# The first two score steps of a dilated attention, issued before the last half of the value projection

## The chip, the cores and the metric

The kernel runs on one core of a Trainium2 chip. Its time is the device time of one execution in microseconds (us). Five engines work side by side: PE multiplies matrices, ACT (ScalarE) applies functions and copies, DVE (VectorE) and POOL (GpSimd) work element by element, and SP starts the transfers from memory. Each engine runs its own instructions in the order in which they were written, and waits on counters (semaphores) that other engines raise.

## The reference

Two model blocks run one after the other over 512 tokens of width 1024. The second block holds, as its second layer, a dilated attention with three groups (window and dilation differ) of eight heads each; the change lies in it alone.

```python
def dilated_attention_mixer(h, positions, w_qkv, w_o):
    qkv = (h @ w_qkv).reshape(b_, s_, 3, g_ * hh, dh)
    q = partial_rotary(qkv[:, :, 0], positions).reshape(b_, s_, g_, hh, dh)
    k = partial_rotary(qkv[:, :, 1], positions).reshape(b_, s_, g_, hh, dh)
    v = qkv[:, :, 2].reshape(b_, s_, g_, hh, dh)
    for g, (window, dilation) in enumerate(DILATED_PATTERNS):
        o_g, lse_g = dilated_window_attention(q[:, :, g], k[:, :, g], v[:, :, g], window, dilation)
    weights = jax.nn.softmax(jnp.stack(lses, axis=0), axis=0)
    o = jnp.sum(weights[..., None] * jnp.stack(outs, axis=0), axis=0)
    return o.reshape(b_, s_, hh * dh).astype(h.dtype) @ w_o
```

Each group's outputs are weighted by the share of its sum of exponentials in the sum over the three groups, so that the kernel takes one softmax over the 768 scores that a block of 128 queries has in the three groups together.

## The kernel before

**The weights.** All weights come as 216 slabs of 1 MB (`w_stage`). POOL splits each slab into a high part (`w_high`, line 410) and a low part (`w_low`, line 415), four instructions each; there are two buffers, and a slab is split into the buffer of the slab before the last as soon as PE has done with that one (`slab_done`). PE makes each product out of three matmuls (lines 473 to 475, function `triple`).

**The attention.** The heads are done in two batches of four. For each batch PE takes twelve slabs of queries and keys, which DVE scales, rotates and stores in `qk2` (named qk in rows of the profile; `head_ready` counts them), and then six slabs of values, two halves for each group `g`. The four banks 4 to 7 of `psum` hold a group's values for the four token blocks `c`; they are complete when the second half is, and ACT then copies each of them to `v_tok` (lines 1252 and 1253), which raises `drained[4 + c]`.

**The steps.** Then come 16 steps of a batch (`t`, four heads by four blocks of queries). For each step
- PE computes the scores into two of the banks 0 to 3 (lines 920 to 922; even steps take 0 and 1, odd steps 2 and 3),
- DVE adds the mask and takes the row maxima (lines 1790 to 1798) into `sc2` (named scores in rows),
- ACT takes the exponential (line 1260),
- DVE divides by the sum (lines 1778 and 1779),
- PE transposes the six blocks of probabilities into banks 4 and 5 (line 945),
- ACT copies them out (`pt2`, line 1268),
- PE multiplies them with the values (line 936).

PE's order in one round `t` is scores of `t`, values of `t - 2`, transposes of `t - 1`. DVE's order is division of `t - 1`, maxima of `t`. ACT's order is exponential of `t`, copy of `t - 1`. Ahead of the first round PE waits for the batch's heads and for `drained` of banks 7, 1, 3 and 5: for bank 7, that is the copy of the last block of values.

Of the kernel before, what the change touches and what calls it, by code (L numbers as in the profile page):

```python
# [28 lines left out]
ACT = mybir.ActivationFunctionType  # L29
# [3 lines left out]
P = 128  # L33
# [8 lines left out]
GROUPS, GHEADS = 3, 8  # L42
BATCH_HEADS = 4
# [113 lines left out]
def build(nc, a):  # L157

    ctx = ExitStack()
    with ctx:  # L160
# [309 lines left out]
        def _(pe):  # L470
# [394 lines left out]
            def attn(p):  # L865
                s0 = p.slab
                for batch in range(2):

                    j0 = 18 * batch
                    if batch == 0:  # L870
                        first_slab(p, (0, 1))
                        plain_slab(p, 1, (2, 3), attn_high, attn_low)
                        turn_rstd(p, 6)
                        done = 2
                    else:
                        done = 0
                    base = [p.drain[b] + used[b] for b in range(4)]
                    if batch:
                        pe.wait_ge(drained[0], base[0])
                        pe.wait_ge(drained[2], base[2])  # L880
                    rounds = (12 - done) // 2
                    with pe.Fori(0, rounds) as i:
                        for r in range(2):
                            s = s0 + j0 + done + r
                            pe.wait_ge(slab_split, i * 2 + (s + 1))
                            slab_two_tiles(s % 2, (2 * r, 2 * r + 1), lambda b: pe.wait_ge(drained[b], i + base[b]), attn_high, attn_low)
                    for b in range(4):
                        used[b] += rounds

                    for g in range(GROUPS):  # L890
                        for half in range(2):
                            s = s0 + j0 + 12 + 2 * g + half
                            pe.wait_ge(slab_split, s + 1)
                            for c in range(TOK):
                                if half == 0:
                                    take(p, 4 + c)
                                for k in range(4):
                                    kk = 4 * half + k
                                    last = triple(ps[:, 4 + c, :], ah[:, kk, c * P:(c + 1) * P], al[:, kk, c * P:(c + 1) * P],
                                                  wh[:, s % 2, k * 512:(k + 1) * 512], wl[:, s % 2, k * 512:(k + 1) * 512],  # L900
                                                  kk == 0, kk == 7)
                                if half == 1 and c < 3:
                                    last.then_inc(tile_done, 1)
                            last.then_inc(slab_done, 1)

                    steps = BATCH_HEADS * DIL
                    n0 = MIX_STEPS + steps * batch
                    pe.wait_ge(head_ready, MIX_HEADS + 24 * (batch + 1))
                    pe.wait_ge(drained[7], p.drain[7] + used[7])
                    pe.wait_ge(drained[1], p.drain[1] + used[1])  # L910
                    pe.wait_ge(drained[3], p.drain[3] + used[3])
                    pe.wait_ge(drained[5], p.drain[5] + used[5])
                    for t in range(steps + 2):
                        if t < steps:
                            h, r = divmod(t, DIL)
                            b = 2 * (t % 2)
                            take(p, b)
                            q = [qk2[:, 4 * g + h, r * P:(r + 1) * P] for g in range(GROUPS)]
                            k = [qk2[:, 12 + 4 * g + h, :] for g in range(GROUPS)]
                            pe.matmul(ps[:, b, :], q[0], k[0], start=True, stop=True)  # L920
                            pe.matmul(ps[:, b + 1, 0:P], q[1], k[1][:, r * P:(r + 1) * P], start=True, stop=True)
                            pe.matmul(ps[:, b + 1, P:2 * P], q[2], k[2][:, r * P:(r + 1) * P], start=True, stop=True) \
                                .then_inc(scores_done, 1)
                        if t >= 2:
                            n = t - 2
                            h, r = divmod(n, DIL)
                            pe.wait_ge(drained[4], p.drain[4] + 19 * batch + 3 + n + 1)
                            b = 6 + h % 2
                            if r == 0:
                                take(p, b)  # L930
                            for kb in range(6):
                                if kb < 4:
                                    v = v2(0, kb)[:, h * P:(h + 1) * P]
                                else:
                                    v = v2(kb - 3, r)[:, h * P:(h + 1) * P]
# [12 lines left out]
                out_projection(p, tiles(o2h), tiles(o2l), lambda k: pe.wait_ge(split_low, split_base_attn() + k + 1))  # L948
# [15 lines left out]
        def _(act):  # L964
# [275 lines left out]
            def attn(p):  # L1240
# [4 lines left out]
                for batch in range(2):  # L1245
                    t0 = p.tile + 21 * batch + 12
                    s0 = p.slab + 18 * batch + 12
                    for g in range(GROUPS):
                        for c in range(TOK):
                            act.wait_ge(*((tile_done, t0 + 3 * g + c + 1) if c < 3 else (slab_done, s0 + 2 * g + 2)))  # L1250
                            if batch == 0:
                                act.wait_ge(drained[6], p.drain[6] + 1)
                            act.activation(v2(g, c), ps[:, 4 + c, :], ACT.Copy, scale=stat[:, 12 + c:13 + c]) \
                                .then_inc(drained[4 + c], 1)
                    steps = BATCH_HEADS * DIL
                    n0 = MIX_STEPS + steps * batch
                    for t in range(steps + 1):
                        if t < steps:
                            act.wait_ge(max_ready, n0 + t + 1)
                            act.activation(sc2[:, t % 2, :], sc2[:, t % 2, :], ACT.Exp, scale=P ** -0.5,  # L1260
                                           bias=stat[:, t % 2:t % 2 + 1], accum_out=stat[:, 2 + t % 2:3 + t % 2]) \
                                .then_inc(exp_ready, 1)
                        if t >= 1:
                            n = t - 1
                            act.wait_ge(probs_turned, n0 + n + 1)
                            if n >= 2:
                                act.wait_ge(values_done, MIX_VALUES + steps * batch + n - 1)
                            act.activation(pt2[:, (n % 2) * 768:(n % 2 + 1) * 768],
                                           ps[:, 4:6, :].rearrange("p b c -> p (b c)")[:, 0:768], ACT.Copy) \
                                .then_inc(drained[4], 1)  # L1270
                            if n % DIL == 2 and n > DIL:
                                o2_copy(p, batch, n // DIL - 1)
                    if batch == 1:

# [702 lines left out]
```

## Time and profile before

| | |
|---|---|
| median of 3 runs (lowest to highest) | 2667.6 us (2667.1 to 2673.45) |
| the profiled execution | 2669.08 us |
| its span in the trace | 2667.3 us |
| PE busy | 2597.1 us, 97% of the span |
| POOL, DVE, ACT busy | 66%, 41%, 19% |
| granted TensorE clock, mean | 0.988 of full speed |

The span runs from the first to the last instruction that the trace shows; the execution has 1.78 us around it. A busy share of 97% says that PE is nearly always at work, not that all of that work has to stand where it stands, and time in which PE runs at the lower clock counts as busy. So two things are read beside it: PE's idle stretches with what ended them, and the granted clock behind them. The clock has two levels here, 2.4 GHz (1.00 in the rows) and 1.2 GHz (0.50).

### The profile page before, as it was taken

How to read it: one execution, taken by the hardware profiler on the slowest of the kernel's cores; microseconds unless marked ns; L12 is line 12 of the kernel's file. 1: busy time of each engine (PE TensorE's matmuls, PEld its weight loads, DVE VectorE, ACT ScalarE, POOL GpSimd, SP SyncE). 2: the span in 40 equal slices, each digit the busy share in tenths (PEclk: the TensorE clock that was granted, in tenths of full speed). 3: DMA queues.
4: the chain of work that ended last, by engine and by line, in shares of the span. 5: the costliest groups of instructions: out<-in, count | busy, mean ns of one | idle time of the engine just before them, and what ended most of it. 6: DMA issues, size and time to landing. Idle time of an engine off the chain costs nothing.

```text
span 2667.3 us, 32279 instructions
## 1 busy us (share of the span) xinstructions
PE 2597.1 (97%) x11906; PEld 2138.4 (80%) x11906; DVE 1082.2 (41%) x1730; ACT 500.6 (19%) x843; POOL 1747.7 (66%) x1761
## 2 busy tenths in 40 slices
PE   7989999999899999999999999999999999999997
PEld 6768888887688888888888888888788878888885
DVE  4753322037533320443521504872567055503325
ACT  3432111034321110201100104100400143100022
POOL 5637777666377776777776876777257615867763
PEclk9999999999999999999999999999999999999998
DMA  4112222231122222222222223223012202222221
GB/s 154 48 48 95 94 96 103 100 117 48 48 95 94 94 95 99 91 99 105 103 95 95 94 95 105 93 97 108 33 63 94 96 31 87 94 95 95 95 95 63
DMA packets 36893, 236.71 MB, mean 89 GB/s; under 512 B 4049, under 2 KB 5585, under 8 KB 9169
## 3 DMA queue, kind: packets, MB, share of 16 engines
q1 hardware_dynamic: 33456, 230.78, 24.7%
q10 hardware_dynamic: 3360, 4.85, 0.6%
q8 instruction: 56, 0.92, 0.1%
q14 instruction: 21, 0.16, 0.0%
HBM read 233.51 MB, written 2.10 MB: 88 GB/s over the span
## 4 chain that ended last, share of the span: by engine, by line
PE 95%; DVE 2%; ACT 1%; issue 1%; POOL 0%; DMA 0%; DVEq 0%; SPq 0%; POOLq 0%; ACTq 0%
PE psum L473 29%; PE psum L474 29%; PE psum L475 29%; PE psum L936 2%; PE psum L920 1%; PE psum L684 1%; PE psum L945 1%; PE psum L798 1%; PE psum L814 0%; PE psum L503 0%; DMA x_res<-in_x 0%; PE psum L830 0%; PE psum L520 0%; PE psum L758 0%; POOL w_low L415 0%
## 5 line engine op out<-in xcount | busy, mean ns | idle before, releaser
L415 POOL TENSOR_TENSOR w_low<-w_stage,w_high 128x512 fp32r<-128x512 f32 x864 | 1145.1, 1356 | 18.0
L410 POOL TENSOR_SCALAR w_high<-w_stage 128x512 fp32r<-128x512 f32 x864 | 573.4, 690 | 861.9 <-PE psum L475 850.5
L473 PE MATMUL psum<-x_high,w_high 128*128 128x512 f32 x1664 | 655.3, 394 | 15.5 <-DVE x_low L1361 15.0
L474 PE MATMUL psum<-x_low,w_high 128*128 128x512 f32 x1664 | 648.8, 390 | 0.0
L475 PE MATMUL psum<-x_high,w_low 128*128 128x512 f32 x1664 | 648.8, 390 | 0.0
L473 PEld LDWEIGHTS psum<-x_high,w_high 128*128 128x128 f32 x1664 | 313.4, 188 | 83.7 <-issue 17.4
L474 PEld LDWEIGHTS psum<-x_low,w_high 128*128 128x128 f32 x1664 | 313.4, 188 | 66.8 <-issue 2.4
L475 PEld LDWEIGHTS psum<-x_high,w_low 128*128 128x128 f32 x1664 | 313.1, 188 | 65.6
L473 PE MATMUL psum<-mlp_high,w_high 128*128 (+1 forms) x576 | 224.1, 389 | 0.0
L474 PE MATMUL psum<-mlp_low,w_high 128*128 (+1 forms) x576 | 224.1, 389 | 0.0
L475 PE MATMUL psum<-mlp_high,w_low 128*128 (+1 forms) x576 | 224.1, 389 | 0.0
L1402 DVE TENSOR_TENSOR psum<-psum,x_res 128x512 f32<-128x512 f32 x56 | 39.2, 700 | 441.1 <-PE psum L475 438.1
L473 PE MATMUL psum<-attn_x_high,w_high 128*128 128x512 f32 x384 | 150.0, 391 | 0.0
L475 PE MATMUL psum<-attn_x_high,w_low 128*128 128x512 f32 x384 | 149.4, 389 | 0.0
L474 PE MATMUL psum<-attn_x_low,w_high 128*128 128x512 f32 x384 | 149.4, 389 | 0.0
L473 PE MATMUL psum<-ffn_high,w_high 128*128 (+1 forms) x352 | 136.9, 389 | 0.0
L474 PE MATMUL psum<-ffn_low,w_high 128*128 (+1 forms) x352 | 136.9, 389 | 0.0
L475 PE MATMUL psum<-ffn_high,w_low 128*128 (+1 forms) x352 | 136.9, 389 | 0.0
L475 PEld LDWEIGHTS psum<-mlp_high,w_low 128*128 128x128 f32 x576 | 108.1, 188 | 22.6
L474 PEld LDWEIGHTS psum<-mlp_low,w_high 128*128 128x128 f32 x576 | 108.1, 188 | 22.4
L473 PEld LDWEIGHTS psum<-mlp_high,w_high 128*128 128x128 f32 x576 | 108.1, 188 | 22.3
L1066 ACT ACTIVATE mlp_high<-work 128x512 f32 x64 | 40.5, 632 | 454.7 <-DVE work L1448 454.7
(271 smaller groups left out, 3377.2 us busy)
## 6 DMA issues: line engine op xcount, KB each, us to landing
w_stage<-in_wstream SPq DMA_DIRECT2D x216, 1024.0 KB, 4.8
x_res<-in_x SPq DMA_DIRECT2D x2, 1024.0 KB, 11.7
out_x<-attn_out SPq DMA_DIRECT2D x8, 256.0 KB, 2.1
inv_count_sb<-in_inv_count ACTq DMA_DIRECT2D x2, 512.0 KB, 8.2
ple_proj<-in_p ACTq DMA_DIRECT2D x2, 512.0 KB, 3.8
qk<-in_mask ACTq DMA_DIRECT2D x1, 576.0 KB, 3.8
w_spat<-in_spatial ACTq DMA_DIRECT2D x2, 256.0 KB, 5.3
diag_sb<-in_diag ACTq DMA_DIRECT2D x2, 256.0 KB, 9.3
```

What stands on the lines that cost most here:

```text
L410: last = pool.tensor_scalar(wh[:, s, part], stage[:, s, part], 1.0, 1.0, ALU.mult, ALU.mult)
L415: last = pool.tensor_tensor(wl[:, s, part], stage[:, s, part], wh[:, s, part].bitcast(F32), ALU.subtract)
L473: pe.matmul(out, wa, ra, start=start, stop=False)
L474: pe.matmul(out, wa, rb, start=False, stop=False)
L475: return pe.matmul(out, wb, ra, start=False, stop=stop)
L684: last = pe.matmul(ps[:, 6, at + c:at + c + 1], W[rows, n % 2, c * P:(c + 1) * P], ones[rows, 0:1], start=True, stop=True)
L798: last = pe.matmul(ps[:, h % 2, kb * P:], vt1[:, kb, h * V_HEAD:(h + 1) * V_HEAD], pt1[:, kb, kb * P:], start=kb == 0, stop=kb == TOK - 1)
L920: pe.matmul(ps[:, b, :], q[0], k[0], start=True, stop=True)
L936: last = pe.matmul(ps[:, b, r * P:(r + 1) * P], v, pt2[:, (n % 2) * 768 + kb * P:(n % 2) * 768 + (kb + 1) * P], start=kb == 0, stop=kb == 5)
L945: last = pe.transpose(ps[:, 4 + kb // 4, (kb % 4) * P:(kb % 4 + 1) * P], sc2[:, n % 2, kb * P:(kb + 1) * P], ident[:])
L1066: act.activation(hh2[:, bass.ds(i * 2 + m, 1), :].rearrange("p a t -> p (a t)"), W[:, 6 + m, :], ACT.Copy).then_inc(hidden_high, 1)
L1402: tt(ps[:, m, :], ps[:, m, :], x[:, m, :], ALU.add).then_inc(x_summed, 1)
```

## The change

The scores of the steps 0 and 1 of each batch become a function, `scores(t)`, and PE issues them between the first and the second half of the last group's value slabs, behind the waits for `head_ready` and for the banks 1 and 3. The loop over the steps then computes scores for steps 2 to 15 only; it still begins with the waits for the banks 7 and 5. ACT takes the exponentials of the steps 0 and 1 ahead of its four copies of the last group's values. DVE's program is the same.

```diff
                     for g in range(GROUPS):
                         for half in range(2):
+                            if (g, half) == (2, 1):
+                                pe.wait_ge(head_ready, MIX_HEADS + 24 * (batch + 1))
+                                pe.wait_ge(drained[1], p.drain[1] + used[1])
+                                pe.wait_ge(drained[3], p.drain[3] + used[3])
+                                scores(0)
+                                scores(1)
                             s = s0 + j0 + 12 + 2 * g + half
                             pe.wait_ge(slab_split, s + 1)
...
-                    pe.wait_ge(head_ready, MIX_HEADS + 24 * (batch + 1))
                     pe.wait_ge(drained[7], p.drain[7] + used[7])
-                    pe.wait_ge(drained[1], p.drain[1] + used[1])
-                    pe.wait_ge(drained[3], p.drain[3] + used[3])
                     pe.wait_ge(drained[5], p.drain[5] + used[5])
                     for t in range(steps + 2):
-                        if t < steps:
...
+                        if 2 <= t < steps:
+                            scores(t)
...
                     for g in range(GROUPS):
+                        if g == 2:
+                            exponential(0)
+                            exponential(1)
                         for c in range(TOK):
...
                     for t in range(steps + 1):
-                        if t < steps:
...
+                        if 2 <= t < steps:
+                            exponential(t)
```

On PE, in the program of before, the last products of the last value slab stand directly ahead of the scores of the steps 0 and 1, and the transposes of step 0 follow (these rows are from the first batch; lines 473 to 475 are the products, 920 to 922 the scores, 945 the transposes):

```order
L473 MATMUL psum<-w_high,attn_x_high 128x512
L474 MATMUL psum<-w_low,attn_x_high 128x512
L475 MATMUL psum<-w_high,attn_x_low 128x512
L920 MATMUL psum<-qk 128x512
L921 MATMUL psum<-qk 128x128
L922 MATMUL psum<-qk 128x128
L920 MATMUL psum<-qk 128x512
L921 MATMUL psum<-qk 128x128
L922 MATMUL psum<-qk 128x128
L945 MATMUL psum<-ident,scores 128x128 x6
```

After the change, from the six score matmuls (now lines 897 to 899) to the transposes (now line 952), with the 48 products of the second half slab between them:

```order
L897 MATMUL psum<-qk 128x512
L898 MATMUL psum<-qk 128x128
L899 MATMUL psum<-qk 128x128
L473 MATMUL psum<-w_high,attn_x_high 128x512
L474 MATMUL psum<-w_low,attn_x_high 128x512
L475 MATMUL psum<-w_high,attn_x_low 128x512
...
L952 MATMUL psum<-ident,scores 128x128 x6
L897 MATMUL psum<-qk 128x512
```

The 48 matmuls of the second half slab have moved to between the scores of step 1 and the transposes of step 0; nothing is added or taken away on PE.

On ACT, before (first batch; line 1253 is the copy of the values, 1260 the exponential, 1268 the copy of the transposed probabilities):

```order
L1253 ACTIVATE v_tok_near<-psum,stat 128x512 x4
L1253 ACTIVATE v_tok_wide<-psum,stat 128x512 x8
L1260 ACT_TABLE_LOAD
L1260 ACTIVATE scores,stat<-scores,stat 128x768 x2
L1268 ACTIVATE probs_t<-psum 128x768
```

And after the change (the copies of the values are line 1272, those of the probabilities line 1282):

```order
L1272 ACTIVATE v_tok_near<-psum,stat 128x512 x4
L1272 ACTIVATE v_tok_wide<-psum,stat 128x512 x4
L1260 ACT_TABLE_LOAD
L1260 ACTIVATE scores,stat<-scores,stat 128x768 x2
L1272 ACTIVATE v_tok_wide<-psum,stat 128x512 x4
L1282 ACTIVATE probs_t<-psum 128x768
```

The load of the table and the first two exponentials have moved ahead of the last four copies of values; the number of table loads is the same.

## Rows read from the trace of the kernel before

**Rows 1.** The page: PE's busy time, share and instructions; the chain that ended last.

```profile
PE 2597.1 (97%) x11906; PEld 2138.4 (80%) x11906; DVE 1082.2 (41%) x1730; ACT 500.6 (19%) x843; POOL 1747.7 (66%) x1761
...
PE 95%; DVE 2%; ACT 1%; issue 1%; POOL 0%; DMA 0%; DVEq 0%; SPq 0%; POOLq 0%; ACTq 0%
```

**Rows 2.** PE's waits, whole span: us in total, times, longest.

```profile
PE psum L945 <- DVE scores L1779: 6.4, 2, 3.2
PE psum L936 <- ACT probs_t L1268: 4.3, 4, 1.3
```

**Rows 3.** Timeline, batch 1, PE: start, duration, instruction [idle before, releaser].

```profile
2134.66 0.39 PE L475 MATMUL psum<-w_high,attn_x_low 128*128 128x512 f32 x1
...
2135.34 0.39 PE L475 MATMUL psum<-w_high,attn_x_low 128*128 128x512 f32 x1
...
2136.55 1.10 PE L920 MATMUL psum<-qk 128*128 128x512 f32 x2 [0.82 <-issue]
...
2137.93 1.02 PE L920 MATMUL psum<-qk 128*128 128x512 f32 x2
...
2142.61 0.88 PE L945 MATMUL psum<-ident,scores 128*128 128x128 f32 x6 [3.21 <-DVE scores L1779]
...
2143.32 1.40 PE L920 MATMUL psum<-qk 128*128 128x512 f32 x2
...
2148.51 1.02 PE L920 MATMUL psum<-qk 128*128 128x512 f32 x2
...
2151.81 1.02 PE L920 MATMUL psum<-qk 128*128 128x512 f32 x2
...
2189.49 1.02 PE L920 MATMUL psum<-qk 128*128 128x512 f32 x2
```

**Rows 4.** Timeline, batch 1, the other engines at the first steps.

```profile
2135.76 0.69 ACT L1253 ACTIVATE v_tok_wide<-psum,stat 128x512 f32<-128x512 f32 x1 [2.03 <-PE psum L475]
2135.98 2.36 POOL L410 TENSOR_SCALAR w_high<-w_stage 128x512 fp32r<-128x512 f32 x4 [3.46 <-PE psum L475]
...
2138.13 0.69 DVE L1790 CUSTOM_DVE_ANT_0 scores<-psum,mask 128x512 f32<-128x512 f32 x1 [64.00 <-PE psum L922]
...
2138.42 5.26 POOL L415 TENSOR_TENSOR w_low<-w_stage,w_high 128x512 fp32r<-128x512 f32 x4
...
2139.58 0.94 ACT L1260 ACTIVATE scores<-scores,stat 128x768 f32<-128x768 f32 x1 [3.13 <-DVE stat L1798]
...
2140.84 1.72 DVE L1779 TENSOR_SCALAR scores<-scores,stat 128x768 f32<-128x768 f32 x1
...
2143.91 0.93 ACT L1260 ACTIVATE scores<-scores,stat 128x768 f32<-128x768 f32 x1 [3.31 <-DVE stat L1798]
...
2152.73 0.62 DVE L1779 TENSOR_SCALAR scores<-scores,stat 128x768 f32<-128x768 f32 x1
```

**Rows 5.** Timeline, batch 0, PE: the same places as in batch 1.

```profile
1876.42 0.39 PE L475 MATMUL psum<-w_high,attn_x_low 128*128 128x512 f32 x1
...
1884.40 1.88 PE L920 MATMUL psum<-qk 128*128 128x512 f32 x2
...
1889.36 1.02 PE L920 MATMUL psum<-qk 128*128 128x512 f32 x2
...
1930.35 1.02 PE L920 MATMUL psum<-qk 128*128 128x512 f32 x2
```

**Rows 6.** Windows: length, PE, PEld, DVE, ACT, POOL busy, granted clock, DMA share, GB/s.

```profile
48.00:59.00 11.00, 11.00 (x55) 10.97 (x55) 4.40 (x12) 2.44 (x4) 1.34 (x2) 0.53 0.27 95
716.00:719.00 3.00, 0.83 (x4) 0.70 (x5) 1.89 (x3) 1.66 (x3) 3.00 (x4) 1.00 0.00 0
1933.00:1940.00 7.00, 4.83 (x40) 4.31 (x39) 1.14 (x6) 3.13 (x6) 0.00 (x0) 1.00 0.00 0
...
2144.00:2146.00 2.00, 1.89 (x6) 1.08 (x6) 0.99 (x3) 1.63 (x3) 0.00 (x0) 0.50 0.53 111
2146.00:2148.00 2.00, 2.00 (x14) 2.00 (x14) 1.04 (x5) 0.85 (x2) 0.00 (x0) 0.69 0.96 406
```

More of the change, by code:

```diff
@@ L888, in attn, with scores @@
                         used[b] += rounds
+                    def scores(t):
+                        h, r = divmod(t, DIL)
+                        b = 2 * (t % 2)
+                        take(p, b)
+                        q = [qk2[:, 4 * g + h, r * P:(r + 1) * P] for g in range(GROUPS)]
+                        k = [qk2[:, 12 + 4 * g + h, :] for g in range(GROUPS)]
+                        pe.matmul(ps[:, b, :], q[0], k[0], start=True, stop=True)
+                        pe.matmul(ps[:, b + 1, 0:P], q[1], k[1][:, r * P:(r + 1) * P], start=True, stop=True)
+                        pe.matmul(ps[:, b + 1, P:2 * P], q[2], k[2][:, r * P:(r + 1) * P], start=True, stop=True) \
+                            .then_inc(scores_done, 1)
                     for g in range(GROUPS):
                         for half in range(2):
+                            if (g, half) == (2, 1):
[4 more added lines that the diff above has]
+                                scores(1)
                             s = s0 + j0 + 12 + 2 * g + half
@@ L907, in attn @@
                     n0 = MIX_STEPS + steps * batch
-                    pe.wait_ge(head_ready, MIX_HEADS + 24 * (batch + 1))
                     pe.wait_ge(drained[7], p.drain[7] + used[7])
-                    pe.wait_ge(drained[1], p.drain[1] + used[1])
-                    pe.wait_ge(drained[3], p.drain[3] + used[3])
                     pe.wait_ge(drained[5], p.drain[5] + used[5])
                     for t in range(steps + 2):
-                        if t < steps:
[L915 to L923, printed above, removed]
+                        if 2 <= t < steps:
+                            scores(t)
                         if t >= 2:
@@ L1247, in attn, with exponential @@
                     s0 = p.slab + 18 * batch + 12
+                    steps = BATCH_HEADS * DIL
+                    n0 = MIX_STEPS + steps * batch
+                    def exponential(t):
+                        act.wait_ge(max_ready, n0 + t + 1)
+                        act.activation(sc2[:, t % 2, :], sc2[:, t % 2, :], ACT.Exp, scale=P ** -0.5,
+                                       bias=stat[:, t % 2:t % 2 + 1], accum_out=stat[:, 2 + t % 2:3 + t % 2]) \
+                            .then_inc(exp_ready, 1)
                     for g in range(GROUPS):
+                        if g == 2:
+                            exponential(0)
+                            exponential(1)
                         for c in range(TOK):
@@ L1254, in attn @@
                                 .then_inc(drained[4 + c], 1)
-                    steps = BATCH_HEADS * DIL
-                    n0 = MIX_STEPS + steps * batch
                     for t in range(steps + 1):
-                        if t < steps:
[L1259 to L1262, printed above, removed]
+                        if 2 <= t < steps:
+                            exponential(t)
                         if t >= 1:
```

## The prediction

> **What bounds the kernel now.** I began with the page's busy shares and its chain: PE is busy for 97% of the span and holds 95% of the chain that ended last [rows 1]. So a change pays if it removes time in which PE idles or runs slowly, and only there. The next view is PE's list of waits. Two of its entries lie in the attention's steps: the transposes waited twice, 3.2 us each, for DVE's division, and the values waited four times, 4.3 us in all, for ACT's copy of the transposed probabilities [rows 2]. The timeline of batch 1 shows where the first of these lies. The last value product starts at 2135.34. PE then stands still until 2136.55, because ACT's copy of the last block of values, from 2135.76 for 0.69, has to empty bank 7 first [rows 3, 4]. It computes two steps of scores and stops again until 2142.61. In that time the chain of step 0 runs through maxima on DVE (2138.13), exponential on ACT (2139.58) and division on DVE (2140.84) [rows 4]. No other PE work stands in the program between.
>
> The windows show a second loss. Behind this wait the granted clock stands at 0.50, 1.2 GHz, from 2144 to 2146 and on the way back to 1.00, 2.4 GHz, from 2146 to 2148, with a mean of 0.69 [rows 6]. The scores of step 2 start at 2143.32 and those of step 3 at 2148.51, 5.19 us later; from step 3 to step 4 it takes 3.30 [rows 3]. In batch 0 the distance from step 2 to step 3 is 4.96 [rows 5]. Both losses are in front of the 12 step intervals that follow, which take 40.98 us together (2148.51 to 2189.49): pairs of 3.30 and 3.53 [rows 3].
>
> **The change, part by part.** *The moved scores* keep their cost. From the start of step 0's to that of step 1's is 1.38 us [rows 3], so two take 2.76 between the half slabs. Going from products to scores and back has no row. Products start (2135.34 - 2134.66) / 3 = 0.227 us apart and last 0.39 each, so that they overlap by 0.16 [rows 3]. If at both passages this overlap is lost, it costs 0.3 us a batch; if nothing is lost, 0. I take 0, because the 1.38 already begins with a restart from a standstill. The waits that moved with the scores are over by then, since DVE had idled for 64.00 us before the first maxima [rows 4], so that every head lies ready.
>
> *The wait of 3.2 us* loses its cause. From the start of step 0's scores to the end of step 1's exponential before takes 2143.91 + 0.93 - 2136.55 = 8.3 us, POOL's interference included [rows 3, 4]. The second half slab has 48 matmuls, 0.227 us apart, and covers 10.9 us. ACT's copies of the last group now stand behind the exponentials. Three of them (3 x 0.69) can follow one another from 8.3 us on, up to 10.4, while the fourth's bank is complete only at 2.76 + 10.9 = 13.7. So there are 3.3 us of reserve, and the fourth copy starts no later after its products than now. The table load of batch 0 still stands directly ahead of the first exponential, where ACT waits for the maxima anyway. The cover of the chain is thus the half slab; without it we have the kernel of before again.
>
> *What stays* is the wait for bank 7, because the loop still opens with it: from the start of the last product to the first instruction behind it 2136.55 - 2135.34 = 1.21 us. Then come the transposes, 2143.32 - 2142.61 = 0.71, then the scores of step 2.
>
> *The clock.* If it holds, the interval from step 2 to step 3 is a steady one. Steps 2 to 15 then have 13 intervals, 7 x 3.30 + 6 x 3.53 = 44.28 us, against 5.19 + 40.98 = 46.17 before in batch 1 and 4.96 + 40.99 = 45.95 in batch 0 [rows 3, 5]. Does it hold through the remaining 0.8 us of idling? No row has just this. The nearest: at the end of batch 0 PE waits twice around transposes, is busy 4.83 of 7.00 us, and the clock stays at 1.00; and a stretch with PE busy 0.83 of 3.00 us, at 716, shows 1.00 too [rows 6]. Before the scores of step 0, the same 0.8 us were followed by full speed [rows 3]. I take it that it holds; the other end is that it falls as before, which keeps 1.89 + 1.67 = 3.6 us of loss.
> The Trainium skill, "TensorE: Matmul & The Clock Gate", section "A second HAM failure mode: psum-queue depth-cycling", speaks against me: short idles between groups of matmuls can let the clock swing down and up again, paid anew each time. By that rule the sum would lose those 3.6 us; the trace agrees with it in part only, as the rows at 1933 and at 716 show idles without a fall [rows 6].
>
> *POOL moves onto the path.* When the last value slab is done, POOL splits the next slab: line 415 starts 2138.42 - 2135.34 = 3.08 us after the last product and runs 5.26 us in four instructions [rows 3, 4]. DVE's division of step 0 met it at 2140.84 and took 1.72; with POOL idle it takes 0.62 [rows 4]. Now the division of step 2 meets it: 1.21 + 0.71 us to step 2's scores, and 2152.73 - 2148.51 = 4.22 from scores to division [rows 3, 4], so it starts 6.14 us after the last product, 3.06 into line 415. The one before started 2.42 into it and came out at 4.14, shortly behind the third instruction's end (3 x 5.26 / 4 = 3.95). If this one comes out there too, it takes 1.08, or 0.46 too long; the bounds are 0 and 1.10. Steps with odd and even numbers each run through maxima, exponential, copy and values with about 0.1 us of reserve, so I charge 0.4 a batch.
>
> *The sum*, from the last product's start to the start of step 15's scores: 2.76 + 1.21 + 0.71 + 44.28 + 0.4 = 49.36 us, with the 2.76 shifting all that follows. Before it was 2189.49 - 2135.34 = 54.15 in batch 1 and 1930.35 - 1876.42 = 53.93 in batch 0. That gives 4.79 + 4.57 = 9.4 us. What follows step 15 is the same chain as before, and PE stays the bound in all that comes later, so the gain reaches the end. The profiled execution took 2669.08 (span 2667.3 and 1.78 around it), which is 1.5 above the median; it would become 2659.7, and the median 2667.6 becomes 2658.2.
>
> **Rivals.** *A: the clock falls all the same* after the wait for bank 7, and the first steps run slowly as now. Gain 9.4 - 3.6 = 5.8, time 2661.8. For it: one fall per batch now, after two waits. Against it: the rows of the windows named above. 14%.
>
> *B: the wait only moves*, since something that the scores need (a head, a free bank, ACT's place in the queue) comes later than I read. Then PE would stand in the middle of the value slabs for as long as it stands now: 2667.6. The 64.00 us of DVE's idling speak against it. 4%.
>
> *C, slower: the clock falls and stays low.* The longest low stretch here, from 48 to 59, has 0.53 over 11 us [rows 6]. In the steps, some 3.3 us of low clock cost 1.89, so 11 us cost about 6.3 a batch. Put at the start of both batches' steps, that takes 12.6 against 9.4: 2670.8. It decides from some 8 us of low clock a batch, and reaches +0.3% only at some 15 us. Against it: the low stretches behind both waits now are about 3 us. 3% for more than 0.3%, 2% for less.
>
> *D: POOL holds DVE longer*, the full 1.10 per batch and the 0.3 of the transitions: gain 9.4 - 1.4 - 0.6 = 7.4, time 2660.2. 12%. In the other direction nothing of POOL's is felt: 9.4 + 0.8 = 10.2, time 2657.4; that is inside the forecast.
>
> **How the numbers follow.** Forecast (8.1 to 10.2 us gained, 2657.4 to 2659.5): 65%, at 2658.2. A 14%, B 4%, C 5%, D 12%. About 0.3%, that is 8.0 us, can be told from no change here. D straddles that bound, and the forecast's lower end is just beyond it, so that some of its weight could be measured as less. Faster by over 0.3%: 65% and a few per cent of D, less what the spread of runs takes (two of three lie within 0.5 us, the third is 5.9 higher): 68%. Within 0.3%: 28%. Slower: 4%. The range goes from 2656.0, 1.4 below the best case, to 2662.8, 1.0 beyond A, so that it takes in the runs' spread; it leaves out B, C and little else.
>
> **What would show it.** In the changed kernel's trace: no wait of line 952 (the transposes) for the division, where there were two of 3.2 us; scores of the steps 0 and 1 about 12 us ahead of the first transposes; a granted clock of 1.00 in the 6 us behind the last value slab; a distance of 3.3 us from step 2 to step 3; the last ACT copy of values 0.7 us long and directly behind its product; a division of step 2 of about 1.1 us. A clock of 0.50 there proves A; a new wait ahead of the first scores proves B; a division of step 2 of 1.7 us proves D. I am wrong if the first transposes wait for DVE again, or if the bank 7 wait grows because ACT's exponentials come late.

## The result, and the profile after

The changed kernel took 2654.22 us (median of four runs, 2654.17 to 2657.48) against 2667.35 (2666.63 to 2673.45) of the kernel before: ratio 0.9947, interval [0.9936, 0.9959]. That is 13.1 us faster. The forecast was 2658.2 with a range from 2656.0 to 2662.8, so the kernel came out 1.8 us below the range. The profiled execution took 2654.21 us, with a span of 2652.4.

First the place of the change. The page and PE's list of waits, after (the rows that answer to [rows 1] and [rows 2]):

```profile
PE 2588.2 (98%) x11906; PEld 2131.0 (80%) x11906; DVE 1080.3 (41%) x1730; ACT 500.2 (19%) x843; POOL 1750.2 (66%) x1761
```

```profile
PE psum L943 <- ACT probs_t L1282: 4.7, 6, 1.3
...
PE psum L952 <- ACT v_tok_wide L1272: 1.6, 2, 0.8
```

The two waits of 3.2 us for DVE's division are gone. What stands there now is the wait for bank 7, twice 0.8 us. The values' waits for ACT's copy of the probabilities grew a little, from 4.3 us in four waits to 4.7 in six. The timeline of batch 1 on PE shows the whole way (it answers to [rows 3]; L897 are the scores, L952 the transposes, L473 to L475 the products):

```profile
2114.44 0.39 PE L475 MATMUL psum<-w_high,attn_x_low 128*128 128x512 f32 x1
2114.67 1.02 PE L897 MATMUL psum<-qk 128*128 128x512 f32 x2
...
2117.19 0.48 PE L473 MATMUL psum<-w_high,attn_x_high 128*128 128x512 f32 x1
...
2127.98 0.39 PE L475 MATMUL psum<-w_high,attn_x_low 128*128 128x512 f32 x1
...
2129.14 0.87 PE L952 MATMUL psum<-ident,scores 128*128 128x128 f32 x6 [0.78 <-ACT v_tok_wide L1272]
2129.85 1.02 PE L897 MATMUL psum<-qk 128*128 128x512 f32 x2
...
2133.15 1.02 PE L897 MATMUL psum<-qk 128*128 128x512 f32 x2
...
2174.60 1.02 PE L897 MATMUL psum<-qk 128*128 128x512 f32 x2
```

The scores follow the products of the first half slab without an idle moment and the second half slab follows the scores. The interval from step 2 to step 3 is 3.30 us where it was 5.19. The other engines in the same stretch (these answer to [rows 4]):

```profile
2116.17 0.69 DVE L1804 CUSTOM_DVE_ANT_0 scores<-psum,mask 128x512 f32<-128x512 f32 x1 [52.06 <-PE psum L899]
...
2117.62 0.94 ACT L1260 ACTIVATE scores<-scores,stat 128x768 f32<-128x768 f32 x1 [12.94 <-DVE stat L1812]
...
2121.78 0.94 ACT L1260 ACTIVATE scores<-scores,stat 128x768 f32<-128x768 f32 x1 [3.14 <-DVE stat L1812]
...
2122.72 1.25 ACT L1272 ACTIVATE v_tok_wide<-psum,stat 128x512 f32<-128x512 f32 x2
...
2128.40 0.69 ACT L1272 ACTIVATE v_tok_wide<-psum,stat 128x512 f32<-128x512 f32 x1 [2.03 <-PE psum L475]
...
2131.07 5.28 POOL L415 TENSOR_TENSOR w_low<-w_stage,w_high 128x512 fp32r<-128x512 f32 x4
...
2134.07 1.14 DVE L1793 TENSOR_SCALAR scores<-scores,stat 128x768 f32<-128x768 f32 x1
```

Both exponentials are through by 2122.7 under the half slab's products. ACT then makes two copies at once, waits for the products of the other two, and the last copy stands directly behind its products (2128.40 after 2127.98, as 2135.76 after 2135.34 before). The granted clock behind both last half slabs, in batch 0 and batch 1 (windows, columns as in [rows 6]):

```profile
1878.00:1882.00 4.00, 4.00 (x31) 3.37 (x30) 2.80 (x9) 1.73 (x3) 4.00 (x4) 1.00 0.00 0
...
2132.00:2136.00 4.00, 4.00 (x30) 3.37 (x30) 2.77 (x10) 1.72 (x3) 4.00 (x4) 1.00 0.01 4
```

It is 1.00 there, where it was 0.50 and 0.69 in batch 1 before. Batch 0's scores of the steps 0 and 15 stand as far apart as batch 1's:

```profile
1860.39 1.02 PE L897 MATMUL psum<-qk 128*128 128x512 f32 x2
...
1920.33 1.02 PE L897 MATMUL psum<-qk 128*128 128x512 f32 x2
```

To compare stretches, I cut each execution at three places: PE's first product, the place in batch 0 where the last half value slab or the moved scores begin ("the cut"), and the first product of the attention's output projection. In changed kernels the cut is the start of the first score. In the kernel before it is 48 products of 0.227 us ahead of the last product's end, 1876.42 + 0.23 - 10.88 = 1865.77 [rows 5]. The first and the last of the three, before and then after, in the timeline:

```profile
15.04 0.77 PE L473 MATMUL psum<-x_high,w_high 128*128 128x512 f32 x1 [15.04 <-DVE x_low L1361]
...
2198.74 0.47 PE L473 MATMUL psum<-attn_high,w_high 128*128 128x512 f32 x1
```

```profile
14.81 0.77 PE L473 MATMUL psum<-x_high,w_high 128*128 128x512 f32 x1 [14.81 <-DVE x_low L1375]
...
2183.85 0.47 PE L473 MATMUL psum<-attn_high,w_high 128*128 128x512 f32 x1
```

| | first product | opening (first product to cut) | attention (cut to output projection) | rest | span |
|---|---|---|---|---|---|
| before | 15.04 | 1850.73 | 332.97 | 468.56 | 2667.3 |
| after | 14.81 | 1845.58 | 323.46 | 468.55 | 2652.4 |
| difference | 0.23 | 5.15 | **9.51** | 0.01 | 14.9 |

The attention, where the change is, gained 9.51 us; the forecast's sum was 9.4. Another 5.15 us come from the opening, in which both programs issue the same work. The windows show what differs there (columns as in [rows 6]), before and then after:

```profile
45.00:60.00 15.00, 12.36 (x65) 12.33 (x66) 6.35 (x15) 4.91 (x11) 4.34 (x4) 0.66 0.20 70
75.00:95.00 20.00, 20.00 (x89) 15.96 (x89) 18.86 (x36) 8.74 (x14) 7.01 (x8) 0.83 0.10 40
```

```profile
45.00:60.00 15.00, 13.20 (x85) 13.10 (x86) 6.80 (x15) 4.26 (x10) 3.99 (x4) 0.77 0.20 71
75.00:95.00 20.00, 20.00 (x107) 16.55 (x107) 18.54 (x36) 6.73 (x11) 10.10 (x11) 1.00 0.10 31
...
612.00:630.00 18.00, 18.00 (x92) 14.82 (x92) 16.43 (x31) 6.00 (x10) 9.40 (x10) 1.00 0.09 24
```

From 75 to 95 us PE is busy throughout in both, and does 89 matmuls at 0.83 before, 107 at 1.00 after. Counting a window's length times twice what its clock lacks to 1.00, windows of 1 us give 41.0 us at the lower clock in the first 700 us before, and 30.7 after. Half of that difference, 5.1 us, is as much as the openings differ by. Whether that is the change's doing or chance is the first question for the experiments.

### The profile page after: what moved, and what is told of

It is laid out like the page before. It is cut to its first block, busy times and chain, and to the rows that moved or that the text cites. A ratio compares the mean times of both kernels' runs of the same rounds, so it can differ in the third digit from the quotient of the medians.

```text
span 2652.4 us, 32279 instructions
## 1 busy us (share of the span) xinstructions
PE 2588.2 (98%) x11906; PEld 2131.0 (80%) x11906; DVE 1080.3 (41%) x1730; ACT 500.2 (19%) x843; POOL 1750.2 (66%) x1761
## 4 chain that ended last, share of the span: by engine, by line
PE 95%; DVE 2%; ACT 1%; issue 1%; POOL 0%; DMA 0%; DVEq 0%; SPq 0%; POOLq 0%; ACTq 0%
PE psum L473 29%; PE psum L475 29%; PE psum L474 29%; PE psum L943 1%; PE psum L897 1%; PE psum L684 1%; PE psum L952 1%; PE psum L798 1%; PE psum L814 0%; PE psum L503 0%; DMA x_res<-in_x 0%; PE psum L830 0%; PE psum L520 0%; PE psum L758 0%; POOL w_low L415 0%
## 5 line engine op out<-in xcount | busy, mean ns | idle before, releaser
L473 PE MATMUL psum<-x_high,w_high 128*128 128x512 f32 x1664 | 654.5, 393 | 16.0 <-DVE x_low L1375 14.8
L475 PE MATMUL psum<-x_high,w_low 128*128 128x512 f32 x1664 | 648.3, 390 | 0.0
L473 PEld LDWEIGHTS psum<-x_high,w_high 128*128 128x128 f32 x1664 | 312.9, 188 | 83.9 <-issue 17.2
L475 PEld LDWEIGHTS psum<-x_high,w_low 128*128 128x128 f32 x1664 | 312.8, 188 | 65.4
L473 PE MATMUL psum<-mlp_high,w_high 128*128 (+1 forms) x576 | 224.1, 389 | 0.0
L475 PE MATMUL psum<-mlp_high,w_low 128*128 (+1 forms) x576 | 224.1, 389 | 0.0
L473 PE MATMUL psum<-attn_x_high,w_high 128*128 128x512 f32 x384 | 150.0, 391 | 0.0
L475 PE MATMUL psum<-attn_x_high,w_low 128*128 128x512 f32 x384 | 149.4, 389 | 0.0
L473 PE MATMUL psum<-ffn_high,w_high 128*128 (+1 forms) x352 | 136.9, 389 | 0.0
L475 PE MATMUL psum<-ffn_high,w_low 128*128 (+1 forms) x352 | 136.9, 389 | 0.0
L1029 ACT ACTIVATE x_res<-psum 128x512 f32<-128x512 f32 x64 | 38.3, 599 | 465.8 <-DVE psum L1416 459.7
L475 PEld LDWEIGHTS psum<-mlp_high,w_low 128*128 128x128 f32 x576 | 108.1, 188 | 22.5
```

The source lines that it names most:

```text
L473: pe.matmul(out, wa, ra, start=start, stop=False)
L475: return pe.matmul(out, wb, ra, start=False, stop=stop)
L1029: act.activation(x[:, m, :], ps[:, m, :], ACT.Copy)
```

## The experiments

Of each profile the same three stretches were read.

| kernel | median, us (lowest to highest, runs) | ratio, interval | opening | low clock, first 700 us | attention |
|---|---|---|---|---|---|
| before again | 2669.26 (2663.84 to 2675.46, 12) | 1.0003 [0.9992, 1.0013] | 1851.11 | 41.0 | 333.14 |
| changed again | 2659.22 (2655.77 to 2665.41, 6) | 0.9965 [0.9952, 0.9979] | 1851.32 | 41.0 | 323.46 |
| scores only | 2667.36 (2665.43 to 2673.01, 11) | 0.9999 [0.999, 1.0008] | 1852.80 | 44.4 | 330.98 |
| no wait for bank 7 | 2655.92 (2653.99 to 2657.39, 5) | 0.995 [0.9937, 0.9963] | 1850.18 | 41.0 | 321.00 |
| batch 0 only | 2665.59 (1) | | 1850.91 | 41.0 | 329.29 |
| before, wait filled | 2668.31 (1) | | 1851.23 | 41.0 | 331.76 |
| POOL held | 2662.07 (1) | | 1851.09 | 41.0 | 325.28 |
| three edits | 2656.56 (2653.62 to 2664.6, 10) | 0.9961 [0.9949, 0.9973] | 1851.00 | 41.0 | 322.62 |
| opening filled | 2657.87 (2655.02 to 2660.28, 5) | 0.9951 [0.9938, 0.9965] | 1846.06 | 30.7 | 323.45 |
| two edits | 2656.79 (2654.01 to 2657.89, 5) | 0.994 [0.9926, 0.9954] | 1851.02 | 41.0 | 320.07 |
| changed, a third time | 2661.4 (2659.75 to 2663.85, 5) | 0.9959 [0.9945, 0.9972] | 1854.75 | 47.8 | 323.44 |

The rest behind the attention was 468.5 to 468.6 us in every one. The kernel before had medians of 2668.92 (first four), 2668.5 (next four) and 2671.03 (last three) beside these.

**The kernel before, unchanged.**

> The kernel of before, unchanged. Theory 1 (the attention's steps gave the 9.4 us of the sum, and the rest of the 13.1 comes from low-clock stretches in the first two mix layers, which lie elsewhere from one execution to the next): the median is within 3 us of before, single executions scatter by some 3 to 7 us, and in the trace the distance from the first product to the attention's last value product differs from the one read before the change by up to 7 us, with other low-clock stretches. Theory 2 (the change itself, as another program, makes the first layers quicker): executions lie within 1 us, and the opening layers have the low stretches of before, at the same places of the program.

The same program came out between 2663.84 and 2675.46, 11.6 us apart. Three runs had shown 6.4, and 3 to 7 were expected. Its attention differs from the first profile's by 0.17 us and its opening by 0.38. The low stretches lie elsewhere in it, though the program is the same: the mean clock is 0.77 from 45 to 60 us where it was 0.66, and 0.81 from 612 to 630 where it was 1.00, with 41.0 us at the lower clock in all, as before.

**The changed kernel again.**

> The changed kernel once more. Theory 1: the steps of both batches take again what they took (gain of 9.4 to 9.8 in that part), while the opening layers may come out anywhere from 0 to 7 us apart from the first profile of this kernel; the gain over before in the median is 8 to 14 us. Theory 2: 12.5 to 13.5 us again, and an opening part as short as in the first profile.

The attention is the same to 0.01 us, the opening 5.74 longer than in the first profile of this program. So the 5.15 us of the first comparison aren't the change's. What the change is worth shows in the attention, and in the medians as 9.7 us.

**Only PE's order moved.**

> Only PE's and so DVE's part of the change: scores of steps 0 and 1 in front of the last half slab, but ACT takes both exponentials behind its last four copies of values, as before. My theory (the chain maxima, exponential, division has to fit under the half slab): only the first maxima are hidden; the first exponential starts some 1.2 us after the last product, the transposes some 3.3 us after it in place of 1.2, and the second exponential delays the first copy of probabilities by another us. A gain of some 2 us per batch if the clock holds, 0.3 if it falls, so 0.5 to 4 us in all. Rival (PE's order alone does it, ACT's is incidental): 9 us or more.

```diff
-                        if g == 2:
+                        if batch in () and g == 2:
                             exponential(0)
                             exponential(1)
...
-                        if 2 <= t < steps:
+                        if (2 if batch in () else 0) <= t < steps:
                             exponential(t)
```

No batch is in `()`, so that ACT's exponentials stand behind the last four copies again. The timeline of batch 1, first ACT, then PE:

```profile
2140.89 0.69 ACT L1277 ACTIVATE v_tok_wide<-psum,stat 128x512 f32<-128x512 f32 x1 [2.03 <-PE psum L475]
2141.47 0.92 ACT L1265 ACTIVATE scores<-scores,stat 128x768 f32<-128x768 f32 x1
```

```profile
2143.60 0.85 PE L957 MATMUL psum<-ident,scores 128*128 128x128 f32 x6 [2.75 <-DVE scores L1798]
2144.28 1.02 PE L897 MATMUL psum<-qk 128*128 128x512 f32 x2
2146.47 1.16 PE L948 MATMUL psum<-probs_t,v_tok_near 128*128 128x128 f32 x8 [0.72 <-ACT probs_t L1287]
2148.57 1.02 PE L897 MATMUL psum<-qk 128*128 128x512 f32 x2
```

Step 0's scores were issued at 2127.15; in the changed kernel its exponential follows 2.95 us later (2117.62 - 2114.67), which would be 2130.1 here. It starts at 2141.47, because in ACT's queue it stands behind the last copy. PE then waits 2.75 us for the division. In batch 0, where ACT's table load stands behind the copies too (1.28 us), PE waits 4.64 us, and the clock is at 0.50 for 3.4 us behind it. From the cut to step 15's scores batch 1 gains 2.4 us and batch 0 loses 0.4. The attention gains 2.0 us instead of 9.5, too little for the medians to show. The second half of the change, ACT's order, is what makes the first half pay.

**No wait for bank 7.**

> The changed kernel without the wait for bank 7 ahead of the loop over the steps; the first use of bank 7 has a wait of its own, and the first copy of probabilities on ACT stands behind all copies of values. The 0.78 us idle ahead of the first transposes goes: 0.8 to 1.0 us per batch, 1.6 to 2.0 us less in the attention than in the changed kernel. Rival (the division of step 2 then meets POOL's split earlier, or the first copy of probabilities waits for the last copy of values): 0 to 0.8 us in all.

```diff
-                    pe.wait_ge(drained[7], p.drain[7] + used[7])
                     pe.wait_ge(drained[5], p.drain[5] + used[5])
```

The transposes use banks 4 and 5, and the values read `v_tok` only behind them. PE's timeline of batch 1:

```profile
2131.41 0.40 PE L475 MATMUL psum<-w_high,attn_x_low 128*128 128x512 f32 x1
2131.64 0.82 PE L951 MATMUL psum<-ident,scores 128*128 128x128 f32 x6
2132.30 1.02 PE L897 MATMUL psum<-qk 128*128 128x512 f32 x2
```

The transposes start 0.23 us after the last product, where it was 1.16 in the changed kernel. The attention is 2.46 us shorter, more than the 1.6 to 2.0 expected and more than twice the 0.93: the division of step 2 now starts earlier against POOL's split and takes 0.92 us instead of 1.14.

**Batch 0 alone.**

> The change in batch 0 alone; batch 1 as before. Read in the trace, not in the time of one execution, since the opening layers vary. My theory (each batch pays for itself): from the first score to that of step 15 batch 0 takes what it takes in the changed kernel (59.94 us), batch 1 what it took before (52.94), and the attention gains some 4.7 of the 9.5 us. Rival (the clock in batch 1 or the transfers gain from an earlier batch 0): batch 1 differs from before by more than 0.5 us.

```diff
-                            if (g, half) == (2, 1):
+                            if batch in (0,) and (g, half) == (2, 1):
```

(and the same condition at ACT's exponentials and at the loop.) Batch 0 runs as in the changed kernel, 59.94 us from its first score to step 15's, so its gain does not need batch 1's. Batch 1 took 53.89 us, 0.95 more than before (2189.49 - 2136.55 = 52.94), and the attention gained 3.7 us, not the 4.7 expected. The rival's sign, more than 0.5 us of difference in batch 1, is there, but as a loss: the clock was low for 6.8 us, from the last us of the wait of 3.2 on and twice as long as before, and step 2 to step 3 took 5.52. One execution can't tell whether batch 0's change brought that about; the second profile of the kernel before had 3.4 us there again.

**The kernel before with its wait filled.**

> The kernel of before with three extra score matmuls (128x512, into bank 7, whose result nobody reads) in PE's wait of 3.2 us ahead of the first transposes: the wait is filled, nothing is moved, so only the clock can change. Theory as predicted (the slow interval from step 2 to step 3, 5.19 and 4.96 us against 3.30, is the clock's): the interval falls to 3.3 to 3.4 in both batches, a gain of 3.4 to 3.6 us in the attention. Rival (some 1 us of it is the first copy of probabilities, which ACT takes only after the second exponential): the clock stays at 1.00, the interval falls to 4.2 to 4.4 only, a gain of 1.2 to 1.8 us, and the values of step 0 wait for the copy.

```diff
+                        if t == 1:
+                            for _ in range(3):
+                                pe.matmul(ps[:, 7, :], qk2[:, 0, 0:P], qk2[:, 12, :], start=True, stop=True)
```

These extra products, whose results are not used, stand ahead of step 0's transposes. PE's timeline of batch 1, ACT's at the same place, then a window of batch 0:

```profile
2142.55 0.88 PE L948 MATMUL psum<-ident,scores 128*128 128x128 f32 x6 [0.64 <-DVE scores L1782]
2143.26 1.02 PE L920 MATMUL psum<-qk 128*128 128x512 f32 x2
...
2145.63 1.16 PE L936 MATMUL psum<-probs_t,v_tok_near 128*128 128x128 f32 x8 [0.90 <-ACT probs_t L1271]
2147.73 1.02 PE L920 MATMUL psum<-qk 128*128 128x512 f32 x2
```

```profile
2143.86 0.94 ACT L1263 ACTIVATE scores<-scores,stat 128x768 f32<-128x768 f32 x1 [3.31 <-DVE stat L1801]
2144.79 0.79 ACT L1271 ACTIVATE probs_t<-psum 128x768 f32<-128x768 f32 x1
```

```profile
1884.00:1888.00 4.00, 2.98 (x19) 2.31 (x20) 2.77 (x11) 1.72 (x3) 1.19 (x1) 1.00 0.38 117
```

The clock stays at 1.00 in both batches, and the interval from step 2 to step 3 is still 4.47 us in both batches, not 3.30. It is the wait of 0.90 for ACT: its first copy of probabilities (2144.79) stands behind the exponential of step 1 (2143.86), and DVE takes the maxima for that one only behind its division of step 0. The clock's part was 5.19 - 4.47 = 0.72 us in batch 1 and 4.96 - 4.47 = 0.49 in batch 0, and the attention gained just these 1.2. The forecast had put 1.89 and 1.67 down to the clock.

**POOL's split held back.**

> The changed kernel; POOL splits the slab after next (whose split fell on the first divisions) only when the scores of step 4 are done. PE needs that slab some 50 us later. My theory (the 0.46 us by which steps 2 to 15 take longer than 44.28 is DVE's division of step 2 behind POOL): that division takes 0.62 in place of 1.14 us, steps 2 to 15 take 44.3 in place of 44.74, the attention 0.8 to 1.0 us less than in the changed kernel. Rival (the steps are late for another reason, such as the position of the pairs of 3.30 and 3.53): 44.7 again.

```diff
+                split_run(at, n)
+                pool.wait_ge(scores_done, MIX_STEPS + 16 * batch + 5)
+                one(n)
...
```

DVE's divisions of the steps 2 to 5 in batch 0 and POOL's split, in the timeline:

```profile
1885.89 0.62 DVE L1800 TENSOR_SCALAR scores<-scores,stat 128x768 f32<-128x768 f32 x1
1889.19 0.62 DVE L1800 TENSOR_SCALAR scores<-scores,stat 128x768 f32<-128x768 f32 x1
...
1892.72 1.58 DVE L1800 TENSOR_SCALAR scores<-scores,stat 128x768 f32<-128x768 f32 x1
...
1896.92 1.39 DVE L1800 TENSOR_SCALAR scores<-scores,stat 128x768 f32<-128x768 f32 x1
```

```profile
1892.61 5.28 POOL L415 TENSOR_TENSOR w_low<-w_stage,w_high 128x512 fp32r<-128x512 f32 x4
```

Without the split the division of step 2 takes 0.62 us, and the two divisions that the held split meets take 1.58 and 1.39. So it is the split that lengthens them. But steps 2 to 15 take 45.66 us in place of the 44.3 expected, and the attention is 1.8 us longer than with the split left where it was.

**Three edits together.**

> The changed kernel without the wait for bank 7, with POOL held as in the run before, and with the two tiles of batch 1's first slab put into batch 0's last two rounds, where PE waits 1.27 and 0.90 us for copies of probabilities. My theory: against the changed kernel the attention loses 2.5 us by the missing wait for bank 7 (as measured), 0.4 by POOL, and 1.8 to 2.2 in batch 0's last rounds: 4.6 to 5.1 us in all, 14 us against before, a ratio of 0.994 to 0.9955. Rival (batch 1's first slabs only move the wait to DVE, which begins a batch's heads after the last values): 2.5 to 3 us.

To the two edits above (no wait for bank 7, POOL held) came the first two tiles of batch 1's first query slab, issued in the last two rounds of batch 0, where PE waits for ACT's copies:

```diff
...
-                        done = 0
+                        plain_slab(p, j0 + 1, (2, 3), attn_high, attn_low)
+                        done = 2
...
+                        if batch == 0 and t >= steps:
+                            m, nxt = t - steps, s0 + 18
+                            if m == 0:
+                                pe.wait_ge(slab_split, nxt + 1)
+                            take(p, m)
+                            for k in range(8):
+                                last = triple(ps[:, m, :], *blk(nxt % 2, 2 * k + m), attn_high[k], attn_low[k], k == 0, k == 7)
+                            last.then_inc(tile_done if m == 0 else slab_done, 1)
```

The expectation missed, and so did its rival. The attention was 0.84 us shorter than the changed kernel's, and 1.62 longer than without the wait for bank 7 alone. Holding POOL cost 2.55 us here (322.62 - 320.07, the next run), more than the 1.82 above, and of the filling a new wait took most (PE's list of waits):

```profile
PE psum L480 <- DVE qk L1795: 1.5, 1, 1.5
```

**Two edits.**

> The changed kernel without the wait for bank 7 in front of the rounds, and with the first two tiles of batch 1's first query slab in the last two rounds of batch 0, where PE waits for ACT's copies; POOL's split stays where it was. Theory: the two edits add up, as the split that was held in the run before cost 1.6 to 1.8 us of its own: attention 320.2 to 320.6 us, 0.4 to 0.8 below that without the wait alone (321.00), and 2.9 to 3.3 below the changed kernel. Rival: the 1.5 us wait for DVE's rotation of the slab's tiles, which appeared in the run before, eats what the filling gains: attention 320.8 to 321.5 us.

Without POOL's hold, the attention is 320.07 us, 0.93 below that without the bank 7 wait alone and 3.39 below the changed kernel. The tiles fill 1.27 + 0.90 us of waits for ACT at batch 0's end, and the 1.5 us for DVE come in return. This is the shortest attention of all, a little below the 320.2 to 320.6 expected. The medians can't part the two best versions (2656.79 and 2655.92, beside different runs of before).

**The opening's wait filled.**

> The changed kernel with three more matmuls in the first layer, put in front of the one-column sums that wait 2.2 to 2.9 us for DVE's token columns at 47 us; their results are not used. Theory (the 5.15 us between the two first profiles lie in the opening, and are the clock's, which falls or doesn't fall at these early waits of PE): the stretch at 0.50 to 0.70 that begins at 48 to 49 us shortens from 6.8 to 10.2 us of lost-clock time to under 4 or vanishes, the way from the first product to the end of the half slab ahead of the last shrinks from 1845.6 to 1851.3 us by 2 to 5 us, to 1842 to 1848; the attention stays at 323.5 us; median 2651 to 2656. Rival 1: the sums of one column that follow are too little work for the clock, whatever stands ahead of them; then the stretch stays as it is, the opening 1845 to 1852, median 2654 to 2660. Rival 2: the opening's scatter is not the clock's at all; then the opening differs by some us although the stretches at the lower clock are equally long.

```diff
+                        if L == 0:
+                            for _ in range(3):
+                                pe.matmul(ps[:, 7, :], ones[:], x[:, 0, :], start=True, stop=True)
```

The wait for `token_cols` is gone, PE runs through but for 0.14 us at 50, and the clock falls all the same during the one-column sums behind it (timeline, then a window):

```profile
44.70 2.74 PE L711 MATMUL psum<-x_res,ones 128*128 128x512 f32 x6
47.27 4.50 PE L684 MATMUL psum<-ones,work 128*128 128x1 f32 x32
```

```profile
48.00:59.00 11.00, 10.86 (x66) 10.76 (x67) 4.43 (x12) 3.50 (x8) 1.37 (x2) 0.69 0.27 95
```

So this first fall does not need the wait, as the first rival had it: the stretch didn't shorten (from 45 to 60 us the mean clock is 0.77, as in the first profile of the changed kernel). Its opening of 1846.06 us has the same low stretches as that profile, which had the wait, so that the filler can't be given the credit. Its five runs lie from 2655.02 to 2660.28, those of the changed kernel beside them (below) from 2659.75 to 2663.85, but the intervals of the two ratios overlap. Whether the filler makes the short opening more frequent stays open.

**The changed kernel a third time.**

> The changed kernel as it is, in more rounds. Theory: attention 323.46 us to within 0.3, the rest behind it 468.5; what differs between executions lies in the opening, 1845 to 1853 us, and its medians over the runs lie 8.5 to 10.5 us below those of the kernel before, ratio 0.9960 to 0.9970. Rival (the first result's 13.1 us are the change's): ratio 0.9945 to 0.9955.

The attention is 323.44, the opening 1854.75, outside what was expected and 9.2 us longer than in the first profile of the very same program. The windows of this execution, to set beside the two above:

```profile
75.00:95.00 20.00, 20.00 (x80) 16.00 (x80) 18.86 (x35) 7.16 (x12) 7.61 (x9) 0.74 0.03 5
...
612.00:630.00 18.00, 18.00 (x86) 14.44 (x85) 15.41 (x32) 10.07 (x16) 3.49 (x5) 0.81 0.17 60
```

PE is busy all the time, with 80 matmuls where the first profile had 107, and from 612 to 630 the clock falls where it had been 1.00. The medians differ by 9.6 us, as expected; the ratio, 0.9959, lies just below the expected 0.9960 to 0.9970 and above the rival's 0.9945 to 0.9955.

## Why the prediction was wrong, and where it was right

**The step that failed** is the last one of the sum: that the profiled execution's time less the gain gives the time after, with a lower end only 1.4 us below the best case for "the runs' spread". I sized that spread from three runs, two of them 0.5 us apart. The unchanged kernel ranges over 11.6 us in 12 runs, the changed one from 2654.17 to 2665.41 in 15. The first four runs of the changed kernel lay at its lower edge. Its two repetitions had medians of 2659.22 and 2661.4, both in the range, and gained 9.7 and 9.6 us, beside a forecast of 9.4. The scatter is the clock's in the opening: over all profiles the opening goes from 1845.6 to 1854.75 us as the time at the lower clock goes from 30.7 to 47.8, and half of those 17.1 us, 8.6, is nearly all of the 9.2. The mean granted clock of the single runs agrees: of the unchanged kernel's 12 runs the shortest has 0.990 and the longest 0.986. By the same count (twice 0.004 of 2669) that is 21.4 us more at 1.2 GHz, and half of it, 10.7 us, is most of the 11.6. The changed kernel's first four runs have 0.990 to 0.991, its eleven later ones 0.988 to 0.991.

What decides, in one execution, where the clock falls wasn't found; in the one place that was tried it wasn't PE's idle time ahead. Three of the first four runs lie within 0.06 us of each other, and none of the eleven later ones is below 2655.77. Whether that was chance, or something that held for that group of runs, stays open. The chip alone doesn't decide it: "opening filled", "two edits" and "changed, a third time" ran on one chip and show 30.7, 41.0 and 47.8 us.

The Trainium skill, "TensorE: Matmul & The Clock Gate", section "What's actually happening", says that the number of slow matmuls at a kernel's start varies from run to run, and that this costs under 1% of a typical span. The stretches read here lie later, from 48 us on, so they are not what that section describes; their scatter, 11.6 us of 2669, is 0.4%. It was more than the change's own uncertainty.

**The sum was right**, term by term, in batch 1 after:

| term | predicted | measured |
|---|---|---|
| moved scores | 2.76, transitions 0 to 0.3 | 2.65 (2117.19 - 2114.67, and 0.13 lost by the products behind) |
| last product to transposes | 1.21 | 1.16 |
| transposes | 0.71 | 0.71 |
| step 2 to step 15 | 44.28 + 0.4 | 44.75 |
| division of step 2 | 1.08 | 1.14 |
| gain, batch 1 and batch 0 | 4.79 + 4.57 | 4.87 + 4.64 |

The gain of a batch is taken from the cut to step 15's scores: in batch 1 2189.49 - 2124.69 = 64.80 before and 2174.60 - 2114.67 = 59.93 after. One reading was wrong without effect: the forecast let three of ACT's copies follow one another from 8.3 us on. The third waited for its own products, until 11.0 us after the first score, and the fourth came no later for it.

**Its reason for one term was wrong.** *The clock* was to explain 3.6 us, the whole lengthening of the first interval. Filling the wait showed that it explains 1.2; the other 2.3 is ACT's first copy queued behind a late exponential. The change removes both, so the sum didn't suffer. The 1.2 isn't the price of Rival A, though. In the changed kernel PE doesn't wait for ACT's first copy, which ends at 2130.86 where the values start at 2131.16, so a fall would not be hidden behind it as it was before. No run with the whole change showed a fall there, so Rival A's 3.6 us stay untested.

**Rival A** fell: the clock is 1.00 in the windows behind both last half slabs. **Rival B** fell for the change, and is what "scores only" shows: without ACT's order the wait moves and little is gained. **Rival C** fell. **Rival D** fell at its size: the division of step 2 took 1.14 us, near the 1.08 of the forecast, and not 1.7. POOL's part in it is shown by the held split. The bounds of 0.62 and 1.72 held in all changed kernels (0.62 to 1.58).

## What to carry to other kernels

Cut the trace at places that both programs share and compare stretch by stretch before believing a total: here one subtraction parted 9.5 us that came with the change from 5.1 that any execution may win or lose, while medians of a few runs could not. When work is moved ahead on one engine, move the work that answers to it on the next engine's queue too; alone, PE's half of this change gained 2.0 of 9.5 us. And a long interval behind a wait isn't the clock's because the clock is low in it: fill the wait and see what is left.

## What the hardware showed that was not expected

The same program on the same data spent between 30.7 and 47.8 us at 1.2 GHz in its first 700 us, and each us of difference cost about half a us. In the run with the opening filled, PE took 32 one-column matmuls from 47.27 on for 4.50 us, without idle time ahead; the clock was 1.00 up to 50 us and 0.50 from 51 to 57.

A division of 128x768 on DVE, 0.62 us alone, took from 0.85 to 1.72 us where it met POOL's split: 0.92, 1.14, 1.39, 1.58 and 1.72 in the cases above. The Trainium skill, "SBUF — State Buffer", section "Who interferes with whom", tells of a port pair that these two engines share: when DVE runs in a mode that takes this pair too, the engine that comes second is blocked until the first one's instruction ends. The sizes fit that as a bound: the delays, 0.23 to 1.10 us, all lie below one POOL instruction, 5.28 / 4 = 1.32 us. They don't fit it to the letter. In batch 1 after, POOL's third instruction ended at 2131.07 + 3 x 1.32 = 2135.03 and the division at 2135.21, 0.18 us later and not 0.62. No run here shows the port itself, or DVE's mode.
